# Expert gates scattered one by one into a zeroed DRAM array instead of built by one-hot matmuls

## The reference

```python
v1, i1 = lax.top_k(s1, PEER_TOPK)            # 8 heads, 128 keys each side, 16 kept
v2, i2 = lax.top_k(s2, PEER_TOPK)
cand = (v1[..., :, None] + v2[..., None, :]).reshape(...)
top_s, pos = lax.top_k(cand, PEER_TOPK)
idx = jnp.take_along_axis(cand_idx, pos, axis=-1)     # cand_idx = i1 * 128 + i2
gate = jax.nn.softmax(top_s, axis=-1)
u, vv = expert_down[idx], expert_up[idx]
pre = jnp.einsum('td,thkd->thk', xt, u)
act = jax.nn.gelu(pre, approximate=False) * gate
return jnp.einsum('thk,thkd->td', act, vv)
```

## Time and profile before

| | |
|---|---|
| median of 3 runs | 3580.58 us (3580.11 to 3580.69) |
| the profiled execution | 3585.94 us, span 3584.1 us |
| granted TensorE clock, mean | 0.997 of full speed |
| busy share of PE, DVE, ACT, POOL | 99%, 60%, 40%, 57% |
| share of PE in the chain that ended last | 62% |
| DMA engines, attention stage / down stage | about 25% / about 90% busy |

### The profile page before, as it was taken

How to read it: one execution, slowest core, us unless ns; L and a number is a source line. 1 busy time by engine, 2 the same in 40 slices (tenths; PEclk the granted TensorE clock), 3 DMA queues, 4 the chain that set the end, 5 groups by cost and what they waited for, 6 DMA issues and landing times.

```text
span 3584.1 us, 50859 instructions
## 1 busy us (share of the span) xinstructions
PE 3540.5 (99%) x20069; PEld 3218.9 (90%) x20069; DVE 2136.7 (60%) x3752; ACT 1418.0 (40%) x1782; POOL 2025.9 (57%) x696
## 2 busy tenths in 40 slices
PE   7999999999999999999999999999999999999999
PEld 5777777777788888899999999999999999999999
DVE  6333344444685139896666666533577777777774
ACT  5544545555422223333444444333333333333332
POOL 2333333333344434477666666677777777777774
PEclk9999999999999999999999999999999999999999
DMA  3322222222334332388989888899999899999994
GB/s 153 139 101 98 96 95 88 97 82 94 120 141 184 110 116 94 126 309 325 357 324 353 322 337 332 347 346 377 360 361 357 348 348 357 363 358 354 354 353 156
DMA packets 181721, 871.95 MB, mean 243 GB/s; under 512 B 15520, under 2 KB 69024, under 8 KB 90400
## 3 DMA queue, kind: packets, MB, share of 16 engines
q1 hardware_dynamic: 59376, 399.48, 30.2%
q0 software_dynamic: 46224, 336.61, 23.7%
q10 hardware_dynamic: 75936, 133.28, 10.1%
HBM read 805.32 MB, written 69.21 MB: 244 GB/s over the span
## 4 chain that ended last, share of the span: by engine, by line
PE 62%; issue 22%; DVE 6%; POOL 5%; DMA 3%; ACT 1%; DVEq 0%; POOLq 0%; SPq 0%; ACTq 0%
PE ps L1514 59%; POOL w_lo L348 5%; DVE ps L1304 4%; PE ps L1744 2%; DMA expert_rows<-down_rows,idx 1%; DMA w_e_raw<-w_stream 1%; DVE h_dense L1434 1%; POOL w_e_lo L355 1%; DVE expert_rows L1291 0%; PE ps L1678 0%; DMA g_dram<-gate_buf 0%; DVE hn_lo L1134 0%; POOL expert_rows L383 0%; ACT w_e_hi L721 0%; DMA x_raw<-x_t 0%
## 5 line engine op out<-in xcount | busy, mean ns | idle before, releaser
L355 POOL TENSOR_TENSOR w_e_lo<-w_e_raw,w_e_hi 128x2048 fp32r<-128x2048 f32 x256 | 1183.5, 4624 | 521.9 <-ACT w_e_hi L721 520.3
L348 POOL TENSOR_TENSOR w_lo<-w_raw,w_hi 128x2048 fp32r<-128x2048 f32 x115 | 538.5, 4682 | 931.9 <-ACT w_hi L415 931.9
L1514 PE MATMUL ps<-sn_hi,w_e_hi 128*128 128x352 f32 x2048 | 669.5, 327 | 7.9 <-POOL w_e_lo L355 5.2
L1514 PE MATMUL ps<-act_hi,w_e_hi 128*128 128x352 f32 x2048 | 664.7, 325 | 5.3 <-DVE h_dense L1434 3.2
L1514 PE MATMUL ps<-act_lo,w_e_hi 128*128 128x352 f32 x2048 | 661.5, 323 | 0.0
L1514 PE MATMUL ps<-act_hi,w_e_lo 128*128 128x352 f32 x2048 | 661.4, 323 | 0.0
L1514 PE MATMUL ps<-sn_hi,w_e_lo 128*128 128x352 f32 x2048 | 661.0, 323 | 0.0
L1514 PE MATMUL ps<-sn_lo,w_e_hi 128*128 128x352 f32 x2048 | 658.7, 322 | 0.0
L721 ACT ACTIVATE w_e_hi<-w_e_raw 128x2048 fp32r<-128x2048 f32 x256 | 489.3, 1911 | 197.6 <-DMA w_e_raw<-w_stream 123.4
L1291 DVE SCALAR_TENSOR_TENSOR expert_rows<-expert_rows,ps 128x2048 f32<-128x2048 f32 x160 | 363.3, 2284 | 202.6 <-DMA expert_rows<-down_rows,idx 112.2
L1514 PE MATMUL ps<-xn_hi,w_hi 128*128 128x512 f32 x1088 | 447.2, 411 | 18.1 <-DVE xn_lo L922 18.0
(11 more groups left out here) (257 smaller groups left out, 4850.5 us busy)
## 6 DMA issues: line engine op xcount, KB each, us to landing
w_e_raw<-w_stream SPq DMA_DIRECT2D x256, 1024.0 KB, 8.1
w_raw<-w_stream SPq DMA_DIRECT2D x116, 1024.0 KB, 4.8
gel_dram<-gel_all ACTq DMA_DIRECT2D x32, 704.0 KB, 9.5
g_dram<-gate_buf ACTq DMA_DIRECT2D x11, 2048.0 KB, 13.2
gel_in<-gel_dram ACTq DMA_DIRECT2D x32, 704.0 KB, 6.3
g_exp<-g_dram ACTq DMA_DIRECT2D x32, 704.0 KB, 14.5
gate_dram<-g_raw ACTq DMA_DIRECT2D x32, 256.0 KB, 2.0
g_in<-gate_dram ACTq DMA_DIRECT2D x16, 512.0 KB, 6.1
```

The costliest lines, as they stand in the source:

```text
L348: nc.gpsimd.tensor_tensor(wlo[s][:, :], raw[s][:, :], whi[s][:, :].bitcast(F32), ALU.subtract).then_inc(lo_ready, 1)
L355: nc.gpsimd.tensor_tensor(e_lo[j % 4][:, :], e_raw[j % 4][:, :], e_hi[j % 3][:, :].bitcast(F32), ALU.subtract).then_inc(lo_ready, 1)
L1514: m = mm(ps[:, bank, 0:width], lhs[:, w], r, start=(n % (3 * per) == 0), stop=(n % (3 * per) == 3 * per - 1))
```

## The change

The gates of the dense tokens are no longer built on TensorE. `g_dram` becomes one flat array with one element for each (key 2, key 1, dense token), 16384 x 352 in all.

- ScalarE writes zeros into it with eleven stores of 2 MB, taken from the zeroed `bias` tile (VectorE clears it at the start): two in each turn of the loop over attention pairs 3 to 7, one ahead of `pair_b`. ScalarE waits for them before it first loads a bias in `pair_b`.
- After the softmax VectorE computes the 3 x 128 element indices of each partition's tokens, with two scalar_tensor_tensor instructions and two copies; dots 17 to 23 follow behind these instead of around the transposes.
- For each unit (head h, block b of 128 tokens, the last with 96) with h > 0 VectorE adds to each gate the gates of the same expert in earlier heads (`merge`, sixteen instructions), one unit per tile in tiles 20 to 40.
- GpSimd scatters the gates, one indirect DMA for each of 384 (h, b, k), each writing 128 (or 96) single elements of four bytes: one per tile in tiles 20 to 42, six per tile from tile 43 to 103. The units of one block follow one another by waits, so that the summed value is written last.
- VectorE makes the low halves of tiles 43 to 105, 63 of them, which GpSimd leaves out; in its turn t that of tile t + 2, ahead of the rows of the tile.
- TensorE's transposes, its one-hot matmuls, ScalarE's copies of gates and VectorE's one-hots go. The gates are read back as rows of 4 x 352 contiguous elements.

```diff
+UNITS = [(h, b) for h in range(HEADS) for b in range(SPARSE)]
+SCATTERS = [(h, b, k) for h, b in UNITS for k in range(TOPK)]
+SLOW, FAST = 1, 6
+ZEROINGS = 11
+UNIT_TILE = {u: T_GATES + n for n, u in enumerate(UNITS[SPARSE:])}
+T_LOW = max(UNIT_TILE.values()) + 3
+SCATTER_TILE = [T_GATES + n // SLOW if n < SLOW * (T_LOW - T_GATES) else T_LOW + (n - SLOW * (T_LOW - T_GATES)) // FAST
+                for n in range(len(SCATTERS))]
+T_LOW_END = SCATTER_TILE[-1] + 3
...
+            def scatter(h, b, k):
+                if (h, b, k) == (0, 0, 0):
+                    pool.wait_ge(zeroed, 16 * ZEROINGS)
+                if k == 0:
+                    pool.wait_ge(scat_ready, 1 if h == 0 else 2 + UNITS.index((h, b)) - SPARSE)
+                    if h > 0:
+                        pool.wait_ge(scattered[b], 16 * TOPK * h)
+                rows_, c = min(P, TD - P * b), PAIRS * b + TOPK * h + k
+                gate = (merged if h > 0 else tv_all)[0:rows_, c:c + 1]
+                nc.gpsimd.indirect_dma_start(g_dram, bass.IndirectOffsetOnAxis(scat_idx[0:rows_, c:c + 1], 0), gate,
+                                             None).then_inc(scattered[b], 16)
...
             for t in range(2 * EXPERT_TILES):
-                if t + 1 < 2 * EXPERT_TILES:
+                if t + 1 < 2 * EXPERT_TILES and not T_LOW <= t + 1 < T_LOW_END:
+                    if t + 1 == T_LOW_END:
+                        pool.wait_ge(lo_ready, B_DOWN + T_LOW_END)
                     low(t + 1)
...
+                for unit, tile in zip(SCATTERS, SCATTER_TILE):
+                    if tile == t:
+                        scatter(*unit)
...
+            def zero_gates(part):
+                blank_row = bias.rearrange("p h c -> p (h c)").rearrange("p (o c) -> p o c", o=1).to_broadcast([P, 4, 1024])
+                act.dma_start(g_rows[:, bass.ds(4096 * part, 4096)].rearrange("p (o c) -> p o c", o=4),
+                              blank_row).then_inc(zeroed, 16)
...
+            def merge(h, b):
+                row, mine = slice(PAIRS * b, PAIRS * b + TOPK * h), slice(PAIRS * b + TOPK * h, PAIRS * b + TOPK * h + TOPK)
+                for c in range(mine.start, mine.stop):
+                    at_c = PAIRS * (c - mine.start)
+                    vec.scalar_tensor_tensor(out=same[:, at_c:at_c + TOPK * h], in0=scat_ps[:, row], scalar=scat_f[:, c:c + 1],
+                                             in1=tv_all[:, row], op0=ALU.is_equal, op1=ALU.mult,
+                                             accum_out=others_sum[:, c:c + 1])
+                v.drain()
+                vec.tensor_tensor(merged[:, mine], tv_all[:, mine], others_sum[:, mine], ALU.add).then_inc(scat_ready, 1)
+
+            def low_of_tile(j):
+                b = B_DOWN + j
+                v.wait_ge(hi_ready, b + 1)
+                if j == T_LOW:
+                    v.wait_ge(lo_ready, b)
+                vec.tensor_tensor(e_lo[j % 4][:, :], e_raw[j % 4][:, :], e_hi[j % 3][:, :].bitcast(F32),
+                                  ALU.subtract).then_inc(lo_ready, 1)
...
             for t in range(T_GATES, EXPERT_TILES):
-                for n in range(N_GATES):
-                    if GATE_TILE[n] == t:
-                        one_hots(n)
-                        if n == N_GATES - 1:
-                            vec.memset(tv_sum[:, :], 0.0).then_inc(idx_ready, 1)
+                if T_LOW <= t + 2 < T_LOW_END:
+                    low_of_tile(t + 2)
+                for unit in UNITS[SPARSE:]:
+                    if UNIT_TILE[unit] == t:
+                        merge(*unit)
...
             for t in range(EXPERT_TILES):
-                extras = {12 + 24 * k: [lambda n=n: gates(n)]
-                          for k, n in enumerate(n for n in range(N_GATES) if GATE_TILE[n] == t)}
-                if t == 0:
-                    extras = {6: [lambda: key_scores(CT - 1, 1)]}
-                if t == T_TURN:
-                    extras = {24: [turn_values_and_i1]}
-                if t == T_TURN + 1:
-                    extras = {24: [turn_i2]}
+                extras = {6: [lambda: key_scores(CT - 1, 1)]} if t == 0 else None
```

More of the change, by code:

```diff
@@ L51 @@
 T_EXP = 14
-T_TURN = 17
+T_COPY = 19
 T_GATES = 20
-GATE_TILE = [T_GATES + 5 * n // 6 for n in range(N_GATES)]
 EARLY_PAIRS = 6 * TOPK
@@ L256, in build @@
         gel_out = [sem(f"gelu_stored{s}") for s in range(2)]
[L257 removed]
+        tv_sub, tv_exp, tk_done = sem("top_shifted"), sem("top_exp"), sem("topk_done")
         root_ready = sem("h_rstd_columns")
[L259 to L260 removed]
+        blank, zeroed = sem("blank_ready"), sem("gates_zeroed")
+        scat_ready, scattered = sem("scatter_ready"), [sem(f"gates_scattered{b}") for b in range(SPARSE)]
         up_in = [sem(f"up_in{s}") for s in range(2)]
@@ L603, in pair_b @@
                 take_v(2 + n - 8, v_st[:, :])
+            zero_gates(ZEROINGS - 1)
             pair_b(0, 8, "A")
@@ L830, in _ @@
                 peer_hi(t + 2)
-                for n in range(N_GATES):
-                    if GATE_TILE[n] == t:
-                        gates_out(n)
                 down(t)
                 if t == T_FIRST:
-                    act.wait_ge(g_dma, 16 * GATE_GROUPS)
-                    act.wait_ge(idx_ready, 2)
+                    for b in range(SPARSE):
+                        act.wait_ge(scattered[b], 16 * PAIRS)
                     act.wait_ge(gate_x_in, 16 * COPIES)
@@ L1364, in _ @@
             vec.tensor_tensor(per_head(tv_all), per_head(tv_all), one_each(sum_ps), ALU.mult).then_inc(tk_done, 1)
-            for j in range(17, 20):
+            both = slice(0, PAIRS * SPARSE)
+            by_block = lambda t: t[:, both].rearrange("p (b c) -> p b c", b=SPARSE)
+            token = cols[:, C_TOK:C_TOK + SPARSE].rearrange("p (b o) -> p b o", o=1).to_broadcast([P, SPARSE, PAIRS])
+            vec.scalar_tensor_tensor(out=by_block(scat_f), in0=by_block(i1_all), scalar=float(TD), in1=token,
+                                     op0=ALU.mult, op1=ALU.add)
@@ L1366, in _ @@
+            v.drain()
+            vec.scalar_tensor_tensor(out=scat_f[:, :], in0=i2_all[:, both], scalar=float(KEYS * TD), in1=scat_f[:, :],
+                                     op0=ALU.mult, op1=ALU.add)
+            v.drain()
+            vec.tensor_copy(scat_ps, scat_f[:, :])
+            vec.tensor_copy(scat_idx[:, :], scat_f[:, :]).then_inc(scat_ready, 1)
+            vec.tensor_copy(gate_3[:, :], tv_all[:, sparse])
+            for j in range(17, FIRST_ROWS):
                 dot(j)
             v.drain()
-            vec.tensor_copy(gate_3[:, :], tv_all[:, sparse])
@@ L1863, in lay_out @@
     small[:, C_EPS] = EPS
+    small[:, C_TOK:C_TOK + SPARSE] = np.arange(P)[:, None] + P * np.arange(SPARSE)[None, :]
     keys_t = np.stack([a["peer_sub_keys1"][0], a["peer_sub_keys2"][0]], 1).transpose(3, 0, 1, 2).reshape(P, 16 * KEYS)
```

93 lines of the change are left out of this document (16 added, 77 removed).

## The result

| | before | after |
|---|---|---|
| median | 3580.64 us (3580.11 to 3584.74, 4 runs) | 3680.88 us (3679.67 to 3683.15, 4 runs) |
| ratio, 95% interval | | 1.0278 [1.0260, 1.0296] |
| profiled execution, span | 3585.9, 3584.1 us | 3681.8, 3680.0 us |
| granted TensorE clock, mean | 0.997 | 0.976 |

The change makes the kernel 100 us slower; forecast was 3564. The page of the changed kernel shows where at once: busy times (the line that answers to the earlier trace rows), three of the lines of forty slices, and the chain by line.

A forecast was written before the change was run, and what follows sets the result against it. TensorE was taken as the bound wherever gates are made, GpSimd's issuing in tiles 43 to 105 after the change. Terms -79.2 - 0.9 + 62 + 1 = -17 us gave 3564 us; own range 3550 to 3580, 8 in 10 3497 to 3672.

The forecast's parts named there:

- issues at their pitch: Tiles 43 to 105: GpSimd's scatters and gathers, 1.245 us each, take 546 us against TensorE's 484; stall 62 us.
- the product that waited 2.16 us for GpSimd: Earlier trace: VectorE product with two SBUF inputs ended when GpSimd's subtraction ended; taken as evidence that the engines exclude each other.
- the row I set against it: Earlier trace: a gather beside VectorE's 0.28 us product kept its 0.95 us, though they overlapped only 0.1 us.
- gate matmuls gone: Tiles 21 to 92: removing TensorE's gate matmuls and their small waits saves 79.2 us, all on the path.
- tiles 17 to 20: Transposes and first one-hot waits go, but later dots and gathers return about 3.5 us; net gain 0.9 us.
- tiles 21 to 42, merges: VectorE's merges and dots, taken as 7 us per tile, fit under TensorE's 7.68; no loss, upper end 8 us.
- zeroing: Attention stage: eleven stores issued by ScalarE cost 1 us, between 0 and 5.
- Rival 2: Tiles 43 to 105: VectorE's two-SBUF-input low halves hold GpSimd's issues, 1.65 us each, 102 us more, 3666 us; chance 0.25.
- the difference carried over: Whole kernel: the median lies 5 us below the profiled execution, assumed the same after the change.
- Rival 1: Tiles 43 to 105: scatters are cheap to issue, nothing stalls, the whole 80 us gain stays, 3501 us; chance 0.17.
- Rival 3: Scatter stretch: DMA engines can't write single elements to DRAM fast enough; 3636 us at 60 ns a packet; chance 0.13.

The follow-up runs named there:

- the even kernel in pieces: Changed kernel with scatters spread evenly over tiles 20 to 108 and each VectorE low half cut into four instructions: 3503.05 us, ratio to before 0.9782.
- the second run without scatters: Repeat of the changed kernel without its 384 scatter DMAs, gates read back as zero: 3524.05 us, ratio to before 0.9834.

## Why the prediction was wrong

The failed step is in the sum of tiles 43 to 105: I priced an indirect DMA's issue from stretches of the kernel before where no VectorE instruction with two SBUF inputs ran, and put the case where one does among the rivals, at 0.25, and at nothing in the sum. In its place the runs show a hold of 1.46 us for each of VectorE's low halves, 90 us where the whole forecast gain was 17. It isn't the only miss: without the hold, with one input in PSUM, the kernel takes 3589.1 us, over the forecast's own 3550 to 3580, since the term of the issues at their pitch was 22 us too small. I had the two pieces for the hold, the product that waited 2.16 us for GpSimd and GpSimd never idle in this stretch; the row I set against it says nothing either way: that gather began 0.10 us before the product of 0.28 us ended and was done 0.85 us after it, just as a held issue is in the trace of after (0.78 to 0.88 us).

| step | predicted, us | measured, us |
|---|---|---|
| gate matmuls gone, from tile 20 on | -79.2 | -83.8 (739.7 before; 655.9 in the even kernel in pieces) |
| tiles 17 to 20 | -0.9 | +2.35 (+0.2 to +0.7 in six other kernels) |
| tiles 21 to 42, merges | 0 | 0 (167.8, as without scatters) |
| tiles 43 to 106, issues at their pitch | +62 | +84 (the kernel with one input in PSUM) |
| the hold | a rival: +102 | +90 |
| zeroing | +1 | +0.35 (within the scatter of the traces) |
| tiles 107 to 127 and the up stage | 0 | +3.3 |
| sum | -17 | +96 |

- **Gates.** Right; the 4.6 us more are not gates but the pace of clean tiles. At a granted clock of 1.00 they take 7.63, 7.68 or 7.73 us, one value for a long row of tiles, which changes between rows and between traces: in the trace of before 7.63 up to tile 13 and 7.68 behind tile 92, in that of after 7.73, then 7.63 in tiles 20 to 54, and 7.73 behind tile 106; what sets it stays open. Of the +3.3 us behind tile 106, 1.1 us are of this kind too (tiles 107 to 127 take 162.4 in place of 161.3); the 2.1 us of the up stage may be, which isn't shown.
- **Tiles 17 to 20.** Right in mechanism; low by 3 us in the trace of after. Six other kernels with the same code in these tiles took 35.2 to 35.7 us, +0.2 to +0.7, and the second run without scatters 37.1, so 1 to 3 us are missing from the sum, and more than one trace is needed to say how many. In after VectorE's index instruction waited for GpSimd's low half and took 3.25 us, the dots followed late, the gathers with them, and the low half of tile 19 began at 1654.33 in place of 1653.4. It ended near 1658.9 (the record holds it and that of tile 20), and tile 19 was complete 10.7 us after that, at 1669.65. VectorE's timeline, then GpSimd's:

```profile
1641.57 3.25 DVE L1373 SCALAR_TENSOR_TENSOR scat_f<-i_all,cols 128x384 f32<-128x384 f32 x1
```

```profile
1648.96 0.93 POOL L401 DMA_INDIRECT expert_rows<-down_rows,idx  x1 [3.31 <-DVE expert_rows L1296]
...
1654.33 9.07 POOL L360 TENSOR_TENSOR w_e_lo<-w_e_raw,w_e_hi 128x2048 fp32r<-128x2048 f32 x2
```

- **Merges.** Right: sixteen instructions at a pitch of 0.155 us (16 elements) to 0.255 (112), 0.205 in the mean, the lower end of the sum's 0.20 to 0.32. But the addition behind them, with two SBUF inputs, had no term: in 14 of 21 cases it ended 0.04 us after a low half of GpSimd's did. Its 21 instances (min/median/max ns):

```profile
L1395 DVE TENSOR_TENSOR merged<-tv_all,others_sum x21: 174/1003/4083, 1669.1 to 1823.7; 128x16 f32<-128x16 f32 x21
```

- **Issues at their pitch.** The mechanism was right and the term 22 us too small. 555.5 us of issues in place of 540: the pitch is 1.262 in the mean, not 1.245 less what the 96-element ones save, since a scatter of 128 takes 0.97 and a gather 0.98 in this stretch, and a scatter of 96 saves 0.06 (0.91), not 0.09 (128 of the 361 have 96 elements, not 119). The issues begin 1.4 us behind the GELU of tile 42; tile 106 takes 9.3 us from the end of its low half to its GELU, not 7.7, in part at the lower clock; and the 488 us that the stall is counted from have a clean tile of 7.63, 3.4 us over 64 tiles. The pace itself was as forecast: 556 us for 61 iterations are 9.1 us a tile. But it shows as some long tiles, not as even ones, and begins at tile 62 (tile 56 with the hold), where I had about 58.
- **Rival 2, the hold.** Its mechanism and its place were right. It came to 1.46 us for each low half in place of 1.65: 2.29, less the 0.13 of its 0.97 us that a held issue has behind it, less the 0.70 us by which it begins behind the low half in the mean. Its time was 3666, the result 3681; the difference is the pitch's 22 us and the small terms, and 4 us of the difference carried over, less the 12 by which the hold was smaller.
- **Zeroing.** GELU 16 came 0.35 us later in after; in the traces of the kernels changed alike up to there it comes between 1639.5 and 1642.0 us, 0.1 us before to 2.4 us behind that of before, and one trace can't tell the zeroing from their scatter.
- **Rival 1** is refuted by the gap of 0.30 us, the same in all traces, and by the 0.97 us of a scatter. **Rival 3** too: rows land in 7.0 us, and at the full pace the DMA engines carry the scatters without a stall. Its price was wrong as well: a scatter is 32 packets in the trace of after, not the 144 of a gather (sixteen of 32 or 24 bytes, 14 and 12 ns each, and sixteen of 4 bytes, 9 ns): two on each engine in place of nine.
- **The difference carried over** from the profiled execution to the median, 5 us, was wrong by 4: after's profile lies 1 us above its median.

The lower clock is a consequence. Its mean is 0.86 only where TensorE waits, and 1.00 in the kernel with the same scatters and no waits. While GpSimd's stretch sets the time it should cost nothing, which is argued and not tried, but at the stretch's end it does cost something: in after the granted clock was 0.50, the lower of its two levels (1.2 in place of 2.4 GHz), until 2501 us, and tile 106, whose low half was ready at 2496.8, took 10.1 us from there to its GELU. In the kernel with one input in PSUM 3.2 us of such a clock lay behind the low half and it took 9.3. At half the clock these stretches are worth about 2.1 and 1.6 us (an estimate), which leaves 8.0 and 7.7.

## What to carry to other kernels

Before a step moves from GpSimd to VectorE, look at where its operands lie: while a subtraction with two SBUF inputs runs, the next indirect DMA that GpSimd starts waits for its end, and the price on GpSimd's queue is what is left of the subtraction when that issue starts, less the 0.13 us that the issue does beforehand (here 1.46 of 2.29 us in the mean). Cut such an instruction into pieces; one operand from PSUM also ends the hold, but how to get the right operand there was not tried. And fill a queue evenly: compare its load tile by tile with the bound engine's tile, not over the stage; here the same 384 issues cost 84 us bunched, with no hold at all, and nothing spread, with 30 us of hold left.

## What the runs showed of the hardware

- An indirect DMA's issue that begins while VectorE subtracts two SBUF operands is held: in 61 cases it ended 0.78 to 0.88 us after the subtraction did, nearly its whole 0.97 us. One that had begun before the subtraction wasn't held (49 cases, 0.91 to 1.00 us), nor did it hold the subtraction. Beside dots, whose second input is in PSUM, and beside the subtraction with one input there, it kept 0.90 to 1.01.
- A VectorE addition of two SBUF operands (128 x 16) waited for a low half of GpSimd's in 14 of 21 cases and ended 0.04 us after it.
- Issue costs are the same for a scatter and a gather: 0.97 and 0.98 us busy and 0.30 to the next in the dense stretch, 0.91 with 96 indices in place of 128.
- Single-element writes to DRAM, 128 of them 4.3 times a tile, added no stall in a stretch with 349 GB/s of traffic in all. The trace has 32 packets for each such scatter.
- Clean tiles of the same 48 matmuls took 7.63, 7.68 or 7.73 us, all at a granted clock of 1.00.
- The granted clock was 1.00 in stretches where TensorE was 100% busy, 0.86 where waits left it 80%.
